# Router logits taken inside the output projection, shift added by matmuls in the turns, ranks by five wide products

## The chip, the cores and the metric

The program runs on one core of a Trainium2 chip. The metric is the device time of one execution in microseconds, the median of the runs shown. All data are float32. Engines are named as in the profile: PE is TensorE (PEld its weight loads), DVE VectorE, ACT ScalarE, POOL GpSimd, SP the engine that issues most DMAs.

## The reference, cut to what matters

The program is a chain of three model layers on a stream of 512 tokens by 1024 features. The change lies in the third, between the output projection of the mixer and the mixture of experts (MoE). In the kernel's symbols, with g, s and gate the adaptive scale, shift and gate of the layer:

```
h   = h + gate1 * (merged @ w_out)                    # the projection, 1024 x 1024
y   = h * rsqrt(mean(h*h) + eps) * norm2_g * (1 + g)  # norm and scale
y   = y + s                                           # shift
gl  = y @ w_group + b_group      # 4 group logits of a token
el  = y @ w_expert + b_expert    # 32 expert logits of a token
group = argmax(gl);  e1, e2 = top 2 of el inside that group
rank  = how many earlier token-choices took the same expert
out = h + gate2 * (w1 * expert_e1(y) + w2 * expert_e2(y)), then a final norm
```

An expert is `(silu(y @ w_gate) * (y @ w_up)) @ w_down` with 256 hidden features. Tokens are put into blocks of 64 by expert and rank, so the experts start only when every token has its expert and its rank.

## The kernel before, in words

The stream is kept transposed: tile `hT[:, k, :]` holds features 128k to 128k+127 on the partitions and the 512 tokens along the row; `xnT` is the same for the normed stream. Each engine runs one instruction list in program order, and they meet by semaphores. PSUM has eight banks; "tiles" 0, 1, 2, ... rotate over banks 0 to 3 (`open_tile` waits until the one four back is evacuated), 4 to 7 have fixed uses.

In `pe2`, after the 16 product pairs of the merge (`seven_pair`), PE waits until five of the seven products of the last pair are read and then runs the projection: eight tiles of eight matmuls of 128x512 (`dense_tile`, L1635). DVE adds each tile to `hT` (L1333) and ACT squares it. After the last tile this happens in a row:

- PE sums the squares over the partitions by matmuls with ones (`block_sums`, L1655); ACT takes the root (`root`), DVE the reciprocal (L2323), and PE spreads it over all partitions (`spread_inverse`, L1665).
- DVE multiplies the eight tiles by the inverse and by `GS2 = norm2_g * (1 + g)` into `xnT` (`apply_norm`, L2334), ACT adds the shift tile by tile (`shifts`).
- PE makes the 36 logits per token as one product of eight 36-column matmuls over 512 tokens (L803). ACT copies it, and PE turns it to token-major form in four pieces (L1677, `turn4`); DVE adds the bias (L1347) and starts the top-2 selection (L1352 to L1369).
- Behind that, PE turns `xnT` into token rows: 32 transposes of 128x128 in eight tiles, each evacuated by ACT into `XB`, and ACT sends them to the scratch `expert_in_scratch` (L958). Only then do the two exponentials of the router run on ACT.
- With the one-hots ready PE makes the ranks and counts: ten matmuls at L816 and four at L819, each 32 columns wide. DVE turns counts and ranks into slots (L1161 to L1407), with one compare and six compare-and-adds for the number of extra blocks; PE places the tokens in their blocks (L827), DVE writes the row index `X_ROW` (L1423), and POOL gathers the tokens of the first blocks by it (L622).
- PE in the meantime turns `hT` (32 transposes) and spreads the second gate (L832).

The experts follow in 24 slots (L842, L855, L865, L877), each with two experts' weights loaded by SP or gathered by POOL.

The order of the work is that of the lists written out in `pe2`, `act2` and `dve2`; there is no planner.

Of the kernel before, what the change touches and what calls it, by code (L numbers as in the profile page):

```python
# [22 lines left out]
P = 128  # L23
T = 512
# [60 lines left out]
def model_kernel(nc, t, out):  # L85

    ctx = ExitStack()
    with ctx:
# [249 lines left out]
        BR = work[:, 14 * T + 288:14 * T + 324]  # L338
        LGT = work[:, 15 * T:16 * T]
# [323 lines left out]
        def pe2(pe, ct, open_tile, take_chunk, dense_tile, norm_sum_in_rows, turn4, new_xn, attention, seven_pair):  # L663
# [130 lines left out]
            pe.wait_ge(sem("product_read"), 7 * (M_BASE[0] + 15) + 5)  # L794
            for n in range(KD):
# [5 lines left out]
            for k in range(KD):  # L801
                before(k)
                ins = pe.matmul(bank[0:36, :], WR[:, k, :], xnT[:, k, :], start=(k == 0), stop=(k == KD - 1))  # L803
            ins.then_inc(sem("logits"), 1)
            evacuated(pe, ct.tile - 1)
# [85 lines left out]
        def act2(act, ct, act_, take_tile, squares, square_tiles, root, attention, first_of_pair, shifts):  # L891
# [51 lines left out]
            squares(hT, arena(24, KD), first=lambda k: evacuated(act, t0 + k))  # L943
            ct.chunk, ct.tile = ct.chunk + KD, ct.tile + KD
            root()
            shifts(MOD[:, 24:32], KD)
            act.wait_ge(sem("logits"), 1)
            free_bank(act_(LGT[0:36, :], bank_of(ct.tile)[0:36, :], ACT.Copy), ct.tile)
            ct.tile += 1
            ct.tile += 1  # L950
            for a in range(TT):
                for half in range(2):
                    act.wait_ge(sem("h_turned"), 2 * a + half + 1)
                    free_bank(act_(XB[a][:, half * 512:(half + 1) * 512], bank_of(ct.tile)[:, :], ACT.Copy), ct.tile)
# [55 lines left out]
        EXTRA, ENDS, OFFSET, FIRST = [ebuf[:, 1, 128 + NE * j:160 + NE * j] for j in range(4)]  # L1010
        REACHED = ebuf[:, 0, 0:200].rearrange("p (c h) -> p c h", c=8)
# [141 lines left out]
        def dve2(dve, ct, link, take_tile, take_turned, apply_norm, add_to_h, copy_tiles, attention, quarter_sum, combine_pair):  # L1153
# [166 lines left out]
            for p in range(16):  # L1320
# [7 lines left out]
                if p % 4 == 3:  # L1328
                    for h in range(2):
                        V.tensor_tensor(MERGED[:, p // 4 * 2 + h, :], M_OUT[2][:, h, :], M_OUT[3][:, h, :], ADD).then_inc(sem("merged"), 1)  # L1330
            for k in range(KD):
# [6 lines left out]
            apply_norm(GS2, shifted=True)  # L1338
            V.tensor_tensor(G2DIAG.rearrange("p (k n) -> p k n", k=KD), ident[:, :].unsqueeze(1).broadcast_to([P, KD, P]),
                            MOD[:, 40:48].unsqueeze(2).broadcast_to([P, KD, P]), MUL).then_inc(sem("g2_diagonal"), 1)  # L1340
# [4 lines left out]
            ct.tile += 1  # L1345
            n = take_turned()
            free_bank(V.tensor_tensor(LG, bank_of(n)[:, 0:144].rearrange("p (q n) -> p q n", q=TT), BR.unsqueeze(1).broadcast_to([P, TT, 36]), ADD), n)  # L1347
            evacuated(dve, n)

# [31 lines left out]
            ts(FIRST, numbers, float(CAP), MUL)  # L1381
# [1511 lines left out]
```

## Time and profile before

| | us |
|---|---|
| median of 3 runs | 2554.71 |
| lowest, highest | 2551.04, 2558.86 |
| profiled execution, its own time | 2550.86 |
| its span | 2549.1 |
| PE busy | 2432.2 (95%) |
| DVE busy | 1389.8 (55%) |
| ACT busy | 488.9 (19%) |
| POOL busy | 788.0 (31%) |

The span runs from the first instruction to the last. A busy engine is not yet a bound: what sets the time is the chain of work that ended last. All starts below are in us from the start of the span. A float32 matmul has two records in the profile, a transpose on PE one.

### The profile page before, as it was taken

Reading aid. Unit: us, or ns where it says so; the run is one execution under the profiler, and the core shown is the slowest. Engines: PE = TensorE matmul, PEld = TensorE weight load, DVE = VectorE, ACT = ScalarE, POOL = GpSimd, SP = SyncE. Lnnn points to the kernel's source line nnn. Section 1 sums busy time; section 2 is a strip of 40 time slices with the busy share of each in tenths; the row PEclk is TensorE's granted clock in tenths of the full one; section 3 lists DMA queues with packets and bytes.
Section 4 is the critical chain, followed back from the end, with each engine's and each line's share of the span. In section 5 each row is a group of like instructions: output and inputs, shape, how many; then the busy total and the mean of one; then the engine's idle time right before and its main releaser. Section 6 shows DMA issues by size and latency. Waiting matters only on the chain.

```text
span 2549.1 us, 29161 instructions
## 1 busy us (share of the span) xinstructions
PE 2432.2 (95%) x10988; PEld 1589.8 (62%) x10988; DVE 1389.8 (55%) x2449; ACT 488.9 (19%) x1039; POOL 788.0 (31%) x704
## 2 busy tenths in 40 slices
PE   8998999999999999999999998999899999799995
PEld 6875468888864444588888843434557885433331
DVE  5558369877744663453467522798896432411113
ACT  2016121100022330211000112001584000311111
POOL 6410134454555017634454201000101540123331
PEclk9999999999999999899999999999899999799998
DMA  5320247732324223333332233533000336299993
GB/s 141 96 67 1 74 131 216 227 112 83 95 79 134 61 61 120 116 83 87 86 93 83 60 107 94 148 110 93 26 1 23 94 85 223 101 373 375 383 349 150
DMA packets 345970, 321.21 MB, mean 126 GB/s; under 512 B 32892, under 2 KB 319537, under 8 KB 333119
## 3 DMA queue, kind: packets, MB, share of 16 engines
q1 hardware_dynamic: 323340, 268.56, 33.2%
q10 hardware_dynamic: 5216, 27.27, 3.2%
q0 software_dynamic: 17280, 23.54, 2.8%
q8 instruction: 90, 1.47, 0.2%
q14 instruction: 44, 0.36, 0.0%
HBM read 354.52 MB, written 25.17 MB: 149 GB/s over the span
## 4 chain that ended last, share of the span: by engine, by line
PE 92%; DVE 4%; issue 1%; ACT 1%; DMA 1%; POOL 0%; SPq 0%; POOLq 0%; DVEq 0%; ACTq 0%
PE bank L1704 30%; PE bank L1635 25%; PE bank L1743 12%; PE bank L855 7%; PE bank L877 3%; PE bank L1814 2%; PE bank L1863 2%; PE bank L1845 2%; PE bank L842 1%; PE bank L1986 1%; PE bank L1655 1%; PE bank L686 1%; PE bank L723 1%; PE bank L733 1%; DVE work L2499 1%
## 5 line engine op out<-in xcount | busy, mean ns | idle before, releaser
L1635 PE MATMUL bank<-xnT,ring 128*128 128x512 f32 (+2 forms) x736 | 326.1, 601 | 7.6 <-ACT xnT L2055 4.5
L1704 PE MATMUL bank<-xnT,ring 128*128 128x256 f32 x1024 | 255.6, 387 | 8.3 <-ACT xnT L2055 5.9
L1635 PEld LDWEIGHTS bank<-xnT,ring 128*128 128x128 f32 (+2 forms) x736 | 137.2, 188 | 191.6 <-issue 187.2
L1704 PE MATMUL bank<-big,ring 128*128 128x256 f32 x1024 | 242.5, 380 | 0.0
L1704 PEld LDWEIGHTS bank<-xnT,ring 128*128 128x128 f32 x1024 | 196.3, 193 | 41.5 <-issue 10.9
L1704 PEld LDWEIGHTS bank<-big,ring 128*128 128x128 f32 x1024 | 193.9, 190 | 27.2 <-issue 1.2
L2055 ACT ACTIVATE rinv<-bank 128x256 f32<-128x256 f32 (+1 forms) x57 | 22.1, 388 | 792.6 <-PE bank L1704 621.5
L496 POOL TENSOR_TENSOR work<-ring 128x512 f32<-128x512 f32 x32 | 44.0, 1377 | 329.7 <-PE bank L1704 189.8
L2055 ACT ACTIVATE work<-bank 128x512 f32<-128x512 f32 (+2 forms) x195 | 104.7, 568 | 191.9 <-PE bank L1635 115.6
L2055 ACT ACTIVATE big<-bank 128x512 f32<-128x512 f32 (+1 forms) x78 | 41.8, 557 | 446.8 <-PE bank L1635 245.2
L1635 PE MATMUL bank<-big,ring 128*128 128x512 f32 x288 | 125.8, 599 | 0.1
L855 PE MATMUL bank<-big,work 128*64 128x512 f32 x384 | 116.8, 611 | 8.5 <-issue 7.3
L2387 DVE TENSOR_TENSOR xnT<-big 128x512 f32<-128x512 f32 x64 | 65.5, 1024 | 92.9 <-PE bank L1704 92.9
L2055 ACT ACTIVATE work<-work,nmax 128x512 f32<-128x512 f32 (+1 forms) x192 | 105.7, 556 | 35.5 <-DVE nmax L2499 35.4
L1635 PE MATMUL bank<-hT,ring 128*128 128x512 f32 x256 | 110.9, 593 | 0.0
L496 POOL TENSOR_TENSOR selw<-ring 128x512 f32<-128x512 f32 x32 | 42.6, 1331 | 198.9 <-PE bank L1704 190.1
L1434 DVE TENSOR_TENSOR work<-bank,causal 128x256 f32<-128x256 f32 x24 | 10.2, 425 | 165.9 <-ACT causal L2055 165.9
L1635 PEld LDWEIGHTS bank<-big,ring 128*128 128x128 f32 x288 | 55.3, 192 | 69.7 <-issue 68.9
L497 POOL TENSOR_TENSOR ring<-ring 128x512 f32<-128x512 f32 x64 | 94.7, 1480 | 0.0
L516 POOL TENSOR_TENSOR big<-ring 128x512 f32<-128x512 f32 (+1 forms) x16 | 18.1, 1133 | 239.7 <-PE bank L1743 211.2
L855 PEld LDWEIGHTS bank<-big,work 128*64 128x64 f32 x384 | 36.3, 141 | 83.9 <-issue 82.3
L877 PE MATMUL bank<-big,work 128*64 128x512 f32 x320 | 87.6, 598 | 0.6 <-ACT work L2055 0.6
(439 smaller groups left out, 4663.4 us busy)
## 6 DMA issues: line engine op xcount, KB each, us to landing
ring<-in_mlp_w_up_dram SPq DMA_DIRECT2D x64, 512.0 KB, 4.4
ring<-in_mlp_w_down_dram SPq DMA_DIRECT2D x64, 512.0 KB, 4.7
big<-in_moe_w_down_dram SPq DMA_DIRECT2D x32, 1024.0 KB, 9.5
work<-in_ada_w_dram ACTq DMA_DIRECT2D x32, 768.0 KB, 4.8
ring<-in_w_in_dram SPq DMA_DIRECT2D x40, 512.0 KB, 3.8
big<-in_moe_w_gate_dram SPq DMA_DIRECT2D x16, 1024.0 KB, 9.9
big<-in_moe_w_up_dram SPq DMA_DIRECT2D x16, 1024.0 KB, 11.9
ring<-in_moe_w_up_dram SPq DMA_DIRECT2D x16, 1024.0 KB, 14.9
```

Source lines behind the costliest of these rows:

```text
L496: G.tensor_tensor(s1, a21, a22, ALU.add).then_inc(sem("weights_added"), 1)
L497: G.tensor_tensor(a21, a11, a21, ALU.subtract).then_inc(sem("weights_turned"), 1)
L855: ins = pe.matmul(bank[h * CAP:(h + 1) * CAP, :].rearrange("p (g n) -> p g n", g=2), XTB[s % 2][:, k, h * CAP:(h + 1) * CAP], gu[h][:, k], ...
L877: ins = pe.matmul(banks[5 + c][h * CAP:(h + 1) * CAP, :], HTB[s % 2][:, k, h * CAP:(h + 1) * CAP], DN_OF[w][h][:, k * D + c * T:k * D + (c ...
L1635: ins = pe.matmul(bank[0:m, 0:n], w[:, q, :], rhs(k), start=(k == 0), stop=(k == total - 1))
L1704: ins = pe.matmul(product(r), left[r][:, kp, :], rhs(r, kp), start=(first and kp == kps[0]), stop=(last and kp == kps[-1]), skip_group_che ...
L1743: ins = pe.matmul(product(r), left[r][:, k, :], rhs, start=(k == 0), stop=(k == half - 1), skip_group_check=True)
L1814: done.append(pe.matmul(o, q, k[:, 0:width], start=True, stop=not masked, skip_group_check=True))
L1845: ins = pe.transpose(banks[n % 3][:, at:at + P], probs(s, h, qi)[:, kb * P:(kb + 1) * P], ident[:, :])
L1863: ins = pe.matmul(o[h * HD:h * HD + m, kb * P:T], v, probs_turned(s, h, kb), start=(kb == 0 and not prior), stop=(kb == TT - 1 and last_of ...
L2055: return nc.scalar.activation(out_, in_, func, **kw)
L2387: V.tensor_tensor(t1, b12, b11, ALU.subtract).then_inc(sem("quarters"), 1)
```

## The change

- The projection is preceded by a wait for all seven products of the last pair. Three times inside it, after tiles 2, 4 and 6, PE makes the logit matmuls of two finished feature tiles, and the last two after the sums of squares. They read `xnT = GS2 * hT`, which ACT now makes right behind each square; the norm's inverse is not in it. Even and odd tiles go to the rows 0 to 35 and 64 to 99 of bank 5.
- The logits of the shift alone, `s @ w`, are eight 36-wide matmuls into bank 6. `rstd` is turned to one number per token by a 4-wide matmul, and DVE takes the reciprocal as `RINVT`. The turn of the logits adds the two halves by a product with `HALVES`. DVE multiplies by `RINVT` and adds the bias, in two operations.
- `apply_norm`, the spreading of the inverse, and `shifts` are gone here. A root on a constant stands ahead of the squares on ACT.
- The shift as a row on all partitions, divided by the inverse later, comes from two 512-wide matmuls with ones against a diagonal (`SHIFTDIAG`), copied by ACT. In each of the eight turns of `xnT` a one-row matmul, `rstd` of the tokens by that row, 512 wide, opens the bank, and four ordinary matmuls against the identity add the turned blocks. ACT multiplies by `RINVT` as it evacuates.
- Ranks and counts are five matmuls: one of 160 columns, then 128, 96, 64 and 32.
- The number of extra blocks is one compare over 7 x 32 and one reduction. `G2DIAG` is made ahead of the projection.

```diff
-            norm_sum_in_rows(arena(24, KD))
-            before = new_xn()
-            pe.wait_ge(sem("router_loaded"), 64)
+                if n in (2, 4, 6):
+                    logits(n - 2)
+                    logits(n - 1)
+            sum_in_rows(arena(24, KD))
+            for k in range(KD):
+                pe.matmul(banks[6][:, 0:36], MOD[:, 24 + k:25 + k].broadcast_to([P, P]), WR[:, k, :], start=(k == 0), stop=(k == KD - 1))
+            logits(KD - 2)
+            logits(KD - 1).then_inc(sem("logits"), 1)
+            pe.wait_ge(sem("stat_read"), ct.n["norm"])
+            pe.matmul(banks[6][:, 64:68], rstd[:, 0:P], ident[:, 0:P:32], start=True, stop=True, skip_group_check=True).then_inc(sem("inverse_wide"), 1)
...
-            turn4(lambda a: LGT[0:36, a * P:(a + 1) * P], rows_=36)
-
+            for a in range(TT):
+                ins = pe.matmul(bank[:, 36 * a:36 * (a + 1)], LGT[0:100, a * P:(a + 1) * P], HALVES[0:100, :], start=True, stop=True)
+            ins.then_inc(turned, 1)
+            for c in range(2):
+                bank = open_tile()
+                pe.matmul(bank[:, :], ones[:, :], SHIFTDIAG[:, c * T:(c + 1) * T], start=True, stop=True).then_inc(sem("h_turned"), 1)
+            for c in range(2):
+                evacuated(pe, SHIFT_TILE + c)
             for a in range(TT):
                 for half in range(2):
-                    turn4(lambda k: xnT[:, 4 * half + k, a * P:(a + 1) * P], done="h_turned")
+                    bank = open_tile()
+                    pe.matmul(bank[:, :], rstd[32 * a:32 * a + 1, 0:P], SHIFTROW[32 * a:32 * a + 1, half * T:(half + 1) * T], start=True, stop=True, skip_group_check=True)
+                    for k in range(4):
+                        ins = pe.matmul(bank[:, k * P:(k + 1) * P], xnT[:, 4 * half + k, a * P:(a + 1) * P], ident[:, :], start=False, stop=True,
+                                        skip_group_check=True)
+                    ins.then_inc(sem("h_turned"), 1)
...
-            for a in range(TT):
-                for c in range(a + 1):
-                    ins = pe.matmul(bank[:, a * NE:(a + 1) * NE], ones[:, :] if c < a else BEFORE[:, :], RE[3][:, c, :],
-                                    start=(c == 0), stop=(c == a))
+            pe.matmul(bank[:, 0:P + NE], BEFORE[:, :], RE3_ZEROS, start=True, stop=False, skip_group_check=True)
             for c in range(TT):
-                ins = pe.matmul(bank[:, P:P + NE], ones[:, :], RE[3][:, c, :], start=(c == 0), stop=(c == TT - 1))
+                later = TT - c
+                to = bank[:, (c + 1) * NE:(TT + 1) * NE].rearrange("p (a n) -> p a n", a=later)
+                ins = pe.matmul(to, ones[:, :], RE[3][:, c, :].unsqueeze(1).broadcast_to([P, later, NE]), start=False, stop=(c == TT - 1),
+                                skip_group_check=True)
...
+            act_(SSQ[:, 0:1], EPSC, ACT.Sqrt)
+            for k in range(KD):
+                evacuated(act, t0 + k)
+                act_(arena(24, KD)[:, k, :], hT[:, k, :], ACT.Square).then_inc(sem("squares"), 1)
+                act_(xnT[:, k, :], hT[:, k, :], ACT.Identity, scale=GS2[:, k:k + 1]).then_inc(sem("xn"), 1)
...
-            ts(EXTRA, counts, float(CAP), ALU.is_gt)
-            for c in range(2, T // CAP):
-                stt(EXTRA, counts, float(CAP * c), EXTRA, ALU.is_gt, ADD)
+            tt(FULL, counts.unsqueeze(2).broadcast_to([P, NE, T // CAP - 1]), FULL_AT.unsqueeze(1).broadcast_to([P, NE, T // CAP - 1]), ALU.is_gt)
+            link(V.tensor_reduce(EXTRA, FULL, AX, ADD))
```

## Rows read from the trace of the kernel before

**Rows 1.** The page, part 4: the chain that ended last, by engine.
```profile
PE 92%; DVE 4%; issue 1%; ACT 1%; DMA 1%; POOL 0%; SPq 0%; POOLq 0%; DVEq 0%; ACTq 0%
```
**Rows 2.** Timeline of PE: start, duration, line, operation, out<-in, shape, count [idle before].
```profile
2118.09 55.17 PE L1635 MATMUL bank<-work,ring 128*128 128x512 f32 x128
2173.19 2.00 PE L1655 MATMUL bank<-big,ones 128*32 128x128 f32 x64
2177.53 1.16 PE L1665 MATMUL bank<-rinv,ident 128*128 128x128 f32 x8 [2.34 <-DVE rinv L2323]
2180.37 9.99 PE L803 MATMUL bank<-xnT,work 128*36 128x512 f32 x16 [1.68 <-ACT xnT L2055]
2191.05 0.44 PE L1677 MATMUL bank<-ident,work 36*128 36x36 f32 x4 [0.68 <-ACT work L2055]
2191.41 3.99 PE L1677 MATMUL bank<-ident,xnT 128*128 128x128 f32 x32
2198.16 0.41 PE L816 MATMUL bank<-work,before 128*128 128x32 f32 x2 [2.75 <-DVE work L1369]
...
2200.80 1.89 PE L819 MATMUL bank<-work,ones 128*128 128x32 f32 x8
...
2211.42 1.94 PE L827 MATMUL bank<-work 128*128 128x24 f32 x16 [0.74 <-DVE work L1407]
2213.20 3.33 PE L832 MATMUL bank<-work,ones 128*128 128x512 f32 x4
```
**Rows 3.** Timeline of DVE, the same columns.
```profile
2116.77 1.88 DVE L2411 TENSOR_TENSOR work<-bank,work 128x256 f32<-128x256 f32 x5
...
2173.30 0.75 DVE L1333 SCALAR_TENSOR_TENSOR hT<-bank,small,hT 128x512 f32<-128x512 f32 x1 [6.12 <-PE bank L1635]
...
2191.59 0.31 DVE L1347 TENSOR_TENSOR work<-bank,work 128x144 f32<-128x144 f32 x1 [5.12 <-PE bank L1677]
...
2199.70 0.17 DVE L1371 TENSOR_REDUCE small<-work 128x4 f32<-128x16 f32 x1 [1.60 <-ACT small L2055]
...
2202.80 0.19 DVE L1161 TENSOR_SCALAR work<-bank 128x32 f32<-128x32 f32 x1 [1.21 <-PE bank L819]
2203.03 1.32 DVE L1165 SCALAR_TENSOR_TENSOR work<-bank,work 128x32 f32<-128x32 f32 x6
...
2208.06 0.37 DVE L1157 TENSOR_TENSOR work<-work,rows 128x200 f32<-128x200 f32 x1
...
2214.60 0.18 DVE L1423 CAST small<-work 128x24 uint32<-128x24 f32 x1
```
**Rows 4.** Timeline of ACT, the same columns.
```profile
2174.73 1.28 ACT L2055 ACT_TABLE_LOAD   x1
...
2196.59 1.09 ACT L2055 ACTIVATE selw<-bank 128x512 f32<-128x512 f32 x2 [0.40 <-ACT work L2055]
...
2198.06 1.28 ACT L2055 ACT_TABLE_LOAD   x1 [0.39 <-ACT selw L2055]
```
**Rows 5.** Windows, router stretch: length, busy (records) by PE, PEld, DVE, ACT, POOL, clock, DMA.
```profile
2180.00:2184.00 4.00, 3.63 (x5) 0.93 (x6) 4.00 (x7) 4.00 (x7) 0.00 (x0) 0.50 0.00 0
...
2200.00:2203.00 3.00, 3.00 (x17) 3.00 (x17) 1.55 (x9) 0.00 (x0) 0.00 (x0) 0.50 0.00 0
...
2206.00:2211.00 5.00, 4.22 (x20) 3.99 (x20) 4.55 (x14) 2.97 (x7) 0.00 (x0) 0.58 0.01 3
```
**Rows 6.** Timeline of PE early in the program: matmuls of eight rows.
```profile
174.88 9.62 PE L1925 MATMUL bank<-work,selw 8*128 8x512 f32 x16
```
**Rows 7.** Windows of that stretch: length, PE busy (records), clock, DMA share, GB/s.
```profile
176.00:178.00 2.00, 2.00 (x6) 1.00 0.00 0
...
180.00:182.00 2.00, 2.00 (x4) 0.50 0.00 0
```
**Rows 8.** Timeline of PE in the expert slots.
```profile
2234.17 7.09 PE L855 MATMUL bank<-ring,work 128*64 128x512 f32 x32 [1.18 <-ACT work L2055]
...
2252.45 0.59 PE L855 MATMUL bank<-hT,work 128*64 128x512 f32 x1
2252.97 0.51 PE L865 MATMUL bank<-ident,work 128*128 128x128 f32 x2
```

More of the change, by code:

```diff
@@ L338, in model_kernel @@
         BR = work[:, 14 * T + 288:14 * T + 324]
+        BIAS = work[:, 14 * T + 324:14 * T + 360]
+        HALVES = work[:, 14 * T + 360:14 * T + 396]
+        SHIFTDIAG, SHIFTROW, RINVT = work[:, 8 * T:10 * T], work[:, 18 * T:20 * T], small[:, 596:600]
+        SHIFT_TILE = 194
         LGT = work[:, 15 * T:16 * T]
@@ L794, in pe2, with logits @@
             pe.wait_ge(sem("product_read"), 7 * (M_BASE[0] + 15) + 5)
+            before = new_xn()
+            def logits(k):
+                before(k)
+                at = 64 * (k % 2)
+                return pe.matmul(banks[5][at:at + 36, :], WR[:, k, :], xnT[:, k, :], start=(k < 2), stop=(k >= KD - 2), skip_group_check=True)
+            pe.wait_ge(sem("router_loaded"), 64)
+            pe.wait_ge(sem("product_read"), 7 * (M_BASE[0] + 16))
             for n in range(KD):
                 dense_tile([KD], lambda k: MERGED[:, k, :], before=(lambda k: pe.wait_ge(sem("merged"), k + 1)) if n == 0 else None)
-            norm_sum_in_rows(arena(24, KD))
@@ L798, in pe2 @@
-            before = new_xn()
-            pe.wait_ge(sem("router_loaded"), 64)
-            bank = open_tile()
[L801 to L805, printed above, removed]
-            turn4(lambda a: LGT[0:36, a * P:(a + 1) * P], rows_=36)
+                if n in (2, 4, 6):
+                    logits(n - 2)
+                    logits(n - 1)
@@ L942, in act2 @@
             t0 = ct.tile
-            squares(hT, arena(24, KD), first=lambda k: evacuated(act, t0 + k))
+            act_(SSQ[:, 0:1], EPSC, ACT.Sqrt)
[3 more added lines that the diff above has]
+                act_(xnT[:, k, :], hT[:, k, :], ACT.Identity, scale=GS2[:, k:k + 1]).then_inc(sem("xn"), 1)
             ct.chunk, ct.tile = ct.chunk + KD, ct.tile + KD
             root()
-            shifts(MOD[:, 24:32], KD)
             act.wait_ge(sem("logits"), 1)
-            free_bank(act_(LGT[0:36, :], bank_of(ct.tile)[0:36, :], ACT.Copy), ct.tile)
+            act_(LGT[0:100, :], banks[5][0:100, :], ACT.Copy).then_inc(sem("logits"), 1)
             ct.tile += 1
-            ct.tile += 1
+            act.wait_ge(sem("rinv"), ct.n["norm"])
+            for c in range(2):
+                act.wait_ge(sem("h_turned"), c + 1)
+                free_bank(act_(SHIFTROW[:, c * T:(c + 1) * T], bank_of(ct.tile)[:, :], ACT.Copy), ct.tile)
+                ct.tile += 1
             for a in range(TT):
                 for half in range(2):
-                    act.wait_ge(sem("h_turned"), 2 * a + half + 1)
-                    free_bank(act_(XB[a][:, half * 512:(half + 1) * 512], bank_of(ct.tile)[:, :], ACT.Copy), ct.tile)
+                    act.wait_ge(sem("h_turned"), 2 * a + half + 3)
+                    free_bank(act_(XB[a][:, half * 512:(half + 1) * 512], bank_of(ct.tile)[:, :], ACT.Copy, scale=RINVT[:, a:a + 1]), ct.tile)
                     ct.tile += 1
@@ L1337, in dve2 @@
             ct.step("squares", KD)
[L1338 to L1340 removed]
+            ct.step("norm")
             link(V.memset(RI[0][:, 0:1], 1000.0))
@@ L1344, in dve2 @@
                 ts(RI[0][:, 1 << lv:2 << lv], RI[0][:, 0:1 << lv], float(1 << lv), ADD)
-            ct.tile += 1
+            dve.wait_ge(sem("router_loaded"), 64)
+            dve.wait_ge(sem("inverse_wide"), ct.step("wide"))
+            V.reciprocal(RINVT, banks[6][:, 64:68]).then_inc(sem("rinv"), 1)
+            link(V.tensor_tensor(BIAS, banks[6][:, 0:36], BR, ADD))
+            dve.wait_ge(sem("rinv"), ct.n["norm"])
             n = take_turned()
-            free_bank(V.tensor_tensor(LG, bank_of(n)[:, 0:144].rearrange("p (q n) -> p q n", q=TT), BR.unsqueeze(1).broadcast_to([P, TT, 36]), ADD), n)
+            tt(LG, bank_of(n)[:, 0:144].rearrange("p (q n) -> p q n", q=TT), RINVT.unsqueeze(2).broadcast_to([P, TT, 36]), MUL)
+            free_bank(V.tensor_tensor(LG, LG, BIAS.unsqueeze(1).broadcast_to([P, TT, 36]), ADD), n)
             evacuated(dve, n)
+            ct.tile += 2
+            link(V.memset(RE3_ZEROS[:, P:P + NE], 0.0))
             def one_hot(logits, n, top, out_, scratch, c):
```

17 lines of the change are left out of this document (14 added, 3 removed).

## The prediction

> **What bounds the kernel now.** I read the chain that ended last first: PE carries 92% of it [rows 1], so a cut on another engine pays only where PE waits. I then looked for PE's waits around the edited lines in its timeline. The projection ends at 2118.09 + 55.17 = 2173.26 [rows 2]; call that moment E. From there to the last index, 2214.60 + 0.18 = 2214.78 or E + 41.5 [rows 3], the work is a relay between engines, and PE sits idle 2.34, 1.68, 0.68, 2.75 and 0.74 us in it [rows 2]. The experts' token gather hangs on that index, so the stage after it moves rigidly with it. The weights of the first slots lie there already. The question is thus where the index comes after the change.
>
> The relay before: the root waits for a table load of 1.28 [rows 4], the inverse is spread by E + 5.4 (2177.53 + 1.16), the logits take 9.99 from 2180.37 [rows 2], and the bias operation starts at 2191.59, E + 18.3 [rows 3]. The ranks end at 2200.80 + 1.89 = 2202.69 [rows 2], and the first step behind them starts at 2202.80, E + 29.5 [rows 3].
>
> **Up to the projection's end.** PE now also waits for the last products of the merge. The last read ends at 2116.77 + 1.88 = 2118.65 [rows 3], where PE started at 2118.09 [rows 2]: 0.6 later. A pair of logit matmuls goes to two column groups. In the experts 32 records of such pairs take 7.09 [rows 8], 0.43 for two records side by side, so a pair costs 0.86 (one behind the other: 1.72, the upper bound). The array changes from one shape of tile to another before and after. Price from a row: the last 64-column record starts at 2252.45, at 0.43 the next would be 2252.88, and the first 128-column one starts at 2252.97 [rows 8], so 0.09 a change. Three pairs: 3 x (0.86 + 0.18) = 3.1. The projection ends at E + 3.7; call that E'. What DVE does extra ahead of it (the diagonals, 1.2 each) lies in its idle 6.12 between tiles [rows 3]; I cost it at nothing, and without that cover it would be 2.5.
>
> **From there to the logits.** The last tile goes through DVE (0.75) and ACT's square and is ready at E' + 1.47, as before: the table load came then, at 2174.73 [rows 4]. That load is now ahead of the projection, but the stream's scaling sits before the root, 0.6. PE's sums end at E' + 1.9 (2175.19) [rows 2]. Eight shift matmuls of 36 columns: I take 0.12 a record, the pace of the spread (1.16 less a tail of 0.28, over 7 [rows 2]), 16 records, 1.9; to E' + 3.8. The last pair with its changes 1.05, to 4.9. The copy on ACT 0.6 with two handovers, to 5.6. The four-piece turn, 8 records, 1.0, to 6.6. The bias step can start at E' + 6.7 = E + 10.4 against E + 18.3. **The logits come 7.9 earlier.**
>
> **The turns.** Before, they were 32 records in 3.99 [rows 2] and PE then waited 2.75 for the one-hots. The selection takes 6.5 and stays. In the changed list PE first makes the shift row, two 512-wide matmuls, 1.72, to E' + 8.3, and waits for ACT to copy the second, 0.65: E' + 9.0. Then eight tiles. The one-row matmul is 512 wide; 16 records of eight-row ones of that width took 9.62 [rows 6], of which about half at the lower clock [rows 7], which fits 0.43 a record at the upper level and 0.86 at the lower, so few rows save nothing: 0.86. Four ordinary matmuls are eight records where transposes were four: 8 x 0.12 = 0.96. Two changes of tile shape, 0.18. A tile is 2.0, eight 16.0, and the turns end at E' + 25.1 = E + 28.8, where they ended at 2195.40, E + 22.1, before. Bounds: 0.5 a tile if it cost what transposes did (4.0 in all), 3.6 a tile at half clock (29 in all). I take 2.0 because its rows are of the same width.
>
> Now what was hidden is late. The one-hots are ready by E' + 13.6 and wait. On ACT the two exponentials stand behind the last of the eight evacuations: it ends 0.65 after the turns; in the trace the last one ended at 2196.59 + 1.09 = 2197.68 [rows 4] and DVE went on at 2199.70 [rows 3], 2.0 for a DMA issue, a table load of 1.28 [rows 4] and the two exponentials. DVE then had 1.9 of small steps and now has 2.2 (the table of limits and a memset). So the step behind the ranks starts 0.65 + 2.0 + 2.2 = 4.9 after the turns, at E + 33.7, **4.2 later than before.** The five wide products (records of at most 160 columns, 1.3 in place of 2202.69 - 2198.16 = 4.5 [rows 2]) are done 3.5 before that and give nothing.
>
> **Behind the ranks.** Seven compares took 0.19 + 1.32 with gaps, 2202.80 to 2204.35, and a memset 0.1 [rows 3]. Two operations of 224 elements replace them, about 0.4 each by the 0.37 of one with 200 [rows 3]: 0.9 saved. PE turns the residual right behind the ranks and is then idle for some 7 us until the block placement. After PE's idle stretches the clock stood at 0.50 (2200 to 2203 [rows 5]), the 1.2 GHz level, and 32-column records cost 0.21 there (8 in 1.89) against 0.12. The placement's 16 records took 1.94 and were waited for [rows 2]; at the lower level 3.6: +1.7 (0 if the clock stays up).
>
> **The sum.** +4.2 - 0.9 + 1.7 = +5.0, rounded down to +4.5 for the 0.12 pace, which has tails in it. The first expert product met the lower clock before and meets it again: no term. Against the profiled execution: span 2549.1 to 2553.6, own time 2550.86 to 2555.4. That execution lies 3.8 below the median of the runs, 2554.71. The forecast for the median is 2554.7 + 4.5 = 2559.2, call it 2559.
>
> On the clock one rule bears. Turns of 128 rows raised it here: from 2206 PE does nothing but transposes and the stretch to 2211 averages 0.58, so it came back inside it [rows 5]. The Trainium skill, "TensorE: Matmul & The Clock Gate", Part 4, says that transposes in the engine's transpose mode do not count as busy for the clock. By that rule ordinary matmuls in their place would hold the clock in the turns better than before; the trace does not agree, so I give it no gain; with either, the sum above stands, and only the first rival below would be less likely.
>
> **Rivals.**
> (a) The clock falls in the turns. For: matmuls of eight rows left PE busy 2.00 of 2.00 and yet the clock went from 1.00 to 0.50 among them [rows 7], and half of each new tile is a one-row matmul. The stretch ahead, with 36-column work and two waits, is thin too: in such work the clock was 0.50 before [rows 5]. Against: the other half has all rows. Price: 3.6 a tile for 2.0, eight times, 12.8; if it falls after a tile or two, 11. It decides from about the second tile on. Time 2570 to 2572: slower.
> (b) The logit pairs do not run side by side: 4 x 0.86 = 3.4 more, 2562.5. Against: the paired records [rows 8].
> (c) The tiles cost what the transposes did, 4.0, with the one-row matmul beside the others. The turns then end at E' + 13, ACT's copies, 0.55 each, soon after, and DVE goes on near E + 21.7: 7.8 earlier, less 0.9, plus 1.7, so -7.0, 2547.7. For: tiles on different rows can overlap. Against: the four matmuls use all 128 rows and write the same bank.
> (d) The change does not do what it says: a square or the scaling needs another table than the root's, and the load is back, 1.3 more: 2560.3. It joins the forecast's range.
>
> **How the numbers follow.** Chances: forecast with (d) 0.64, (a) 0.20, (b) 0.09, (c) 0.07. 0.3% is 7.7 us, about what a measurement of this kernel can tell from none: no change is 2547.0 to 2562.4. The runs of before spread by 4 to either side, so the forecast gives 0.53 to no change, 0.09 to slower and 0.02 to faster; (a) is slower; (b) splits 0.05 and 0.04; (c) 0.03 no change and 0.04 faster. Together faster 0.06, same 0.61, slower 0.33. The range goes from 2552, which leaves out most of (c), to 2573, which takes in (a); the forecast's own is 2554 to 2564.
>
> **What would show it.** Right: the bias step 6.5 to 8 us after the projection's end; eight turn tiles of 1.9 to 2.1; the exponentials directly behind the last evacuation, and the ranks' product ended while DVE still waits for ACT; the placement's records at 0.21. Wrong: turn tiles of 3.6 at clock 0.50 (a), or of about 0.5 (c); logit records that start 0.43 apart one by one (b); or an index less than E + 40 behind the old E.

## The result, and the profile after

| | before | after |
|---|---|---|
| median (lowest to highest), us | 2554.13 (2551.04 to 2558.86), 6 runs | 2573.85 (2569.97 to 2576.69), 6 runs |
| profiled execution, own time | 2550.86 | 2569.97 |
| its span | 2549.1 | 2568.2 |

The change makes the kernel slower: ratio 1.0074, 95% interval 1.0064 to 1.0085, or 19.7 us by the medians. The forecast was 2559; the measured time is 1.9 above what rival (a) gave (2570 to 2572), and 0.85 above the range's upper end of 2573.

I start where [rows 2] stood, with PE's timeline of the router stretch after (start, duration, line, operation, out<-in, shape, count, and in brackets the idle time before).

```profile
2121.13 20.84 PE L1683 MATMUL bank<-work,ring 128*128 128x512 f32 x48 [0.97 <-DVE work L2459]
2141.89 1.05 PE L804 MATMUL bank<-xnT,work 128*36 128x512 f32 x4
...
2179.78 2.00 PE L1703 MATMUL bank<-big,ones 128*32 128x128 f32 x64
...
2188.98 1.09 PE L834 MATMUL bank<-work,rstd 1*128 1x512 f32 x2 [0.73 <-issue]
2190.00 1.16 PE L836 MATMUL bank<-ident,xnT 128*128 128x128 f32 x8
2191.09 1.27 PE L834 MATMUL bank<-work,rstd 1*128 1x512 f32 x2
2192.29 2.07 PE L836 MATMUL bank<-ident,xnT 128*128 128x128 f32 x8
2194.30 2.07 PE L834 MATMUL bank<-work,rstd 1*128 1x512 f32 x2
2196.30 2.08 PE L836 MATMUL bank<-ident,xnT 128*128 128x128 f32 x8
...
2218.20 0.74 PE L842 MATMUL bank<-work,before 128*128 128x160 f32 x2
2218.73 1.22 PE L846 MATMUL bank<-work,ones 128*128 128x128 f32 x8
...
2231.18 2.02 PE L855 MATMUL bank<-work 128*128 128x24 f32 x16 [0.99 <-DVE work L1455]
```

A turn tile is the one-row product (the two records of L834) and the four ordinary products behind it (the eight records of L836). The first tile costs 2191.09 - 2188.98 = 2.1, as forecast; from the third on each costs 4.0, 2.00 for each of its two groups (2194.30, 2196.30 and so on). The eight run from 2188.98 to 2218.20, 29.2 us. The projection is L1683 now, its sums of squares L1703. E', the moment at which the projection ends and the sums start, is 2179.78.

The windows of that stretch, to be held against [rows 5] and [rows 7] (length; busy time and records of PE, PEld, DVE, ACT, POOL; granted clock; DMA share; GB/s):

```profile
2190.00:2195.00 5.00, 5.00 (x20) 3.54 (x20) 3.24 (x12) 1.28 (x2) 0.00 (x0) 0.69 0.00 0
2195.00:2200.00 5.00, 5.00 (x12) 2.28 (x10) 0.00 (x0) 0.78 (x2) 0.00 (x0) 0.50 0.26 105
...
2220.00:2225.00 5.00, 1.30 (x12) 1.06 (x10) 3.26 (x16) 2.77 (x7) 0.00 (x0) 1.00 0.25 103
```

PE is busy 5.00 of 5.00 and yet the granted clock is 0.50, the 1.2 GHz level, from 2195 to 2215. It is back at 1.00 only when the turns are over. This is the pattern of [rows 7], in a place where the index, the row numbers by which POOL gathers the tokens, hangs on it.

DVE's timeline after, whose rows answer to [rows 3]:

```profile
2186.59 0.31 DVE L1194 TENSOR_TENSOR work<-bank,small 128x144 f32<-128x144 f32 x1 [1.20 <-PE bank L823]
...
2193.30 0.28 DVE L1417 TENSOR_TENSOR work<-work 128x128 f32<-128x128 f32 x1
2221.16 0.17 DVE L1419 TENSOR_REDUCE small<-work 128x4 f32<-128x16 f32 x1 [27.57 <-ACT small L2103]
...
2223.45 0.39 DVE L1194 TENSOR_TENSOR work<-bank,work 128x224 f32<-128x224 f32 x1
...
2234.45 0.18 DVE L1471 CAST small<-work 128x24 uint32<-128x24 f32 x1
```

ACT's timeline after at the end of its copies, which answers to [rows 4]:

```profile
2218.45 0.69 ACT L2103 ACTIVATE selw<-bank,small 128x512 f32<-128x512 f32 x1 [3.32 <-PE bank L836]
...
2219.52 1.28 ACT L2103 ACT_TABLE_LOAD   x1 [0.39 <-ACT selw L2103]
```

DVE has the one-hots at 2193.30 + 0.28 = 2193.58 and then waits 27.57 us for ACT's exponentials. They stand behind the table load, that behind the last evacuation, and that behind the last turn tile. The index is ready at 2234.45 + 0.18 = 2234.63; before it was 2214.78 [rows 3]. That is 19.85 later, of which 2.15 lies ahead of the change's first instruction: the last products of the merge start at 2119.13, and at 2116.98 in the trace of before. This is a difference between two executions; in e6, which is the kernel before up to the ranks, the same products start at 2121.82. The other 17.7 lie between the start of the projection and the index. The profiled spans differ by 19.1, so behind the index nothing more is lost.

### The profile page after: what moved, and what is told of

Its sections match the earlier page's. It is cut to its first block, busy times and chain, and to the rows that moved or that the text cites. A ratio compares the mean times of both kernels' runs of the same rounds, so it can differ in the third digit from the quotient of the medians.

```text
span 2568.2 us, 29256 instructions
## 1 busy us (share of the span) xinstructions
PE 2452.3 (95%) x11036; PEld 1602.2 (62%) x11036; DVE 1389.2 (54%) x2442; ACT 490.8 (19%) x1042; POOL 787.3 (31%) x704
## 4 chain that ended last, share of the span: by engine, by line
PE 93%; DVE 4%; issue 1%; ACT 1%; DMA 1%; POOL 0%; SPq 0%; ACTq 0%; POOLq 0%; DVEq 0%
PE bank L1752 30%; PE bank L1683 25%; PE bank L1791 12%; PE bank L883 7%; PE bank L905 3%; PE bank L1862 2%; PE bank L1893 2%; PE bank L1911 2%; PE bank L870 1%; PE bank L1703 1%; PE bank L2034 1%; PE bank L690 1%; PE bank L727 1%; PE bank L836 1%; PE bank L834 1%
## 5 line engine op out<-in xcount | busy, mean ns | idle before, releaser
L1683 PE MATMUL bank<-xnT,ring 128*128 128x512 f32 (+2 forms) x736 | 327.7, 603 | 6.5 <-ACT xnT L2103 4.5
L1683 PEld LDWEIGHTS bank<-xnT,ring 128*128 128x128 f32 (+2 forms) x736 | 137.4, 189 | 191.9 <-issue 187.8
L2103 ACT ACTIVATE work<-bank 128x512 f32<-128x512 f32 (+1 forms) x191 | 102.7, 567 | 191.0 <-PE bank L1683 115.5
L1683 PE MATMUL bank<-big,ring 128*128 128x512 f32 x288 | 125.8, 599 | 0.1
L2103 ACT ACTIVATE work<-work,nmax 128x512 f32<-128x512 f32 (+1 forms) x192 | 105.7, 556 | 35.2 <-DVE nmax L2547 35.1
L1683 PE MATMUL bank<-hT,ring 128*128 128x512 f32 x256 | 110.9, 593 | 0.0
L1683 PEld LDWEIGHTS bank<-big,ring 128*128 128x128 f32 x288 | 55.3, 192 | 69.7 <-issue 68.9
```

Of the source, the lines that this page charges most:

```text
L1683: ins = pe.matmul(bank[0:m, 0:n], w[:, q, :], rhs(k), start=(k == 0), stop=(k == total - 1))
L2103: return nc.scalar.activation(out_, in_, func, **kw)
```

## The experiments

All times of an experiment stand beside runs of the kernel before on the same chip. In the first three the shift's row in the turns is the question: is it the width of the one-row product, its few rows, or its being there at all?

**e1: all rows.** The same sum, but the factor is a 128-row matrix with `rstd` in one row and zeros elsewhere, made by four small DVE operations.

```diff
-pe.matmul(bank, rstd[32 * a:32 * a + 1, 0:P], SHIFTROW[32 * a:32 * a + 1, ...], start=True, ...)
+pe.matmul(bank, MASKED[:, a * P:(a + 1) * P], SHIFTROW[:, ...], start=True, ...)
```

> The changed kernel with the one-row matmul of each turn tile taken over all 128 rows: its stationary operand is the same row of roots with zeros in the other 127 rows (four small operations on DVE make it). Same width, same number of records, same output. Theory 1 (the clock falls because few rows are active): the clock stays at 1.00 in the turns, a tile costs 0.86 + 0.96 = 1.8, eight 14.6 where they took 29.3, the time falls from 2573.9 to about 2559. Theory 2 (the tiles cost what they cost by their width and their weight loads, and the clock falls in any such mix): the clock falls all the same, a tile stays near 3.6 to 4.0, the time is 2571 or more.

Measured: 2559.18 (2555.29 to 2562.08, 10 runs), ratio 1.0015 (1.0004 to 1.0026). One tile and the start of the next in PE's timeline (timelines and windows have the columns given above in all that follows):

```profile
2194.54 1.02 PE L835 MATMUL bank<-work 128*128 128x512 f32 x2
2195.40 1.05 PE L837 MATMUL bank<-ident,xnT 128*128 128x128 f32 x8
2196.30 1.02 PE L835 MATMUL bank<-work 128*128 128x512 f32 x2
```

A window of the same kernel in the middle of the turns:

```profile
2200.00:2205.00 5.00, 5.00 (x30) 3.57 (x29) 0.00 (x0) 2.06 (x3) 0.00 (x0) 1.00 0.27 108
```

The clock stays at 1.00, a tile costs 1.76, and the time is 14.7 below that of the change (ratio to before 1.0015 against 1.0074) with the same output and as many matmul instructions of the same width. The profiled execution is the slowest of the ten, 2562.08, and its merge ended late (the last products start at 2122.88), so the gain is read from the medians and from the tile. The median is also the forecast's time, within 0.2. So neither the width of the product nor the order of the work brings the clock down. What differs is the rows, and with them the changes of tile shape, which e1 doesn't have; e9 and e10 part the two.

**e2: no row.** The one-row product is taken out and the first turned block opens the bank; the shift is missing from the experts' input, nothing else.

> The changed kernel without the one-row matmuls (the shift is left out of the experts' input; the routing is untouched). Theory 1: clock 1.00, a tile 1.0, eight 8; the turns end some 21 us earlier and the time is about 2553. Theory 2: the clock falls in the ordinary products alone, a tile 2.0, eight 16, about 2561.

Measured: 2549.92 (2548.55 to 2554.27, 10 runs), ratio 0.9992 (0.9982 to 1.0002). All 64 records of the turns are one group:

```profile
2189.97 7.38 PE L835 MATMUL bank<-ident,xnT 128*128 128x128 f32 x64 [0.73 <-issue]
```

That is 0.115 a record and 0.92 a tile, at a clock of 1.00. The product for the shift thus costs 0.84 a tile in e1 (1.76), 1.2 in the change's own form while the clock holds (2.1), and 3.1 in the change's tiles at the lower clock (4.0).

**e3: transposes.** As e2, and the four products are transposes again, as before the change.

> As the run before, and the ordinary products against the identity are transposes again (the shift is left out of the experts' input). What the turns cost in all: both theories put them at 4.0 on PE, held to about 5.5 by the evacuations on ACT of 0.69 each; the index then hangs on the selection and the exponentials, and the time is 2550 to 2552: the logits part of the change alone is worth 3 to 5 us against 2554.1. If this run stays above 2560, the loss is not in the turns.

Measured: 2552.55 (2547.84 to 2556.45, 10 runs), ratio 0.9996 (0.9987 to 1.0006). In its profiled execution the clock was down before the turns and up in them, by PE's timeline:

```profile
2187.62 3.54 PE L828 MATMUL bank<-work,ones 128*128 128x512 f32 x4
2191.89 2.81 PE L835 MATMUL bank<-ident,xnT 128*128 128x128 f32 x24 [0.73 <-issue]
```

The shift row's two products take 3.54 in place of 1.96. In windows of 1 us the clock is 0.60 in 2190 to 2191 and 1.00 from 2191 on, so it was back before the first transpose; the 24 transposes go at 0.117 a record, the upper level, and don't bring it down. Ordinary products need twice the records (7.38 against some 4.3 with PE's waits for ACT's copies), but that lies beside DVE's selection, and the time isn't higher. So the products in place of transposes are not what made the change slow. Whether transposes do less for the clock than ordinary products stays open: e3's executions have mean clocks of 0.969 to 0.974, e2's of 0.973 to 0.976. In the two traces the clock fell in PE's wait for DVE behind the ranks and came back at 2210 to 2211 in e2 and at 2218 in e3; there both kernels run the same instructions, so the difference of the means need not come from the turns.

**e4: rows together.** The turns go by halves; the four one-row products of a half, which lie on rows 0, 32, 64 and 96 and write four banks, are issued one behind the other ahead of the 16 products.

```diff
-for a in range(TT):
-    for half in range(2):
-        bank = open_tile()
-        pe.matmul(bank, <row of a>, ...)
-        <4 products>
+for half in range(2):
+    four = [open_tile() for a in range(TT)]
+    for a in range(TT):
+        pe.matmul(four[a], <row of a>, ...)
+    for a in range(TT):
+        <4 products into four[a]>
```

> The full function. The four one-row matmuls of one half lie on four different row groups and write four banks; here they are issued together and the products follow, so there are 2 groups of four and 4 changes of tile shape in place of 8 single ones and 16. Theory 1: the four run side by side, 0.86 a group, the clock stays up: 2 x 1.05 + 8 x 0.96 = 9.8 in place of 29.3, about 2555. If they run one after the other with the clock up: 15, about 2560. Theory 2 (clock falls in any mix): 19 or more, 2563 or more.

Measured: 2553.08 (2549.52 to 2557.71, 10 runs), ratio 0.9999 (0.9989 to 1.0009). PE's timeline of the turns:

```profile
2189.00 1.14 PE L834 MATMUL bank<-work,rstd 1*128 1x512 f32 x8 [0.78 <-ACT work L2105]
2190.07 3.84 PE L837 MATMUL bank<-ident,xnT 128*128 128x128 f32 x32
2194.78 1.14 PE L834 MATMUL bank<-work,rstd 1*128 1x512 f32 x8 [0.87 <-ACT selw L2105]
```

Eight records of one row each take 1.14 together: the four row groups work side by side, where one product alone took 1.09. The clock is 1.00 in both halves of this execution. PE spends 2 x 1.14 in one-row products, where eight one by one take 8 x 1.09 at this clock, and the loss of 19.7 is gone. That the change has no gain then is a question of its own, taken up in e11.

**e5: 32 rows.** The one-row product reads 32 rows of the same numbers (the row divided by 32), all else as in the change. **e10: 64 rows** is e1 with 64 of its 128 rows, and **e9: two sides** is e1 with the 128-row product written as two of 64 columns side by side.

```diff
-pe.matmul(bank, rstd[32 * a:32 * a + 1, 0:P], SHIFTROW[32 * a:32 * a + 1, ...], ...)
+pe.matmul(bank, rstd[32 * a:32 * a + 32, 0:P], SHIFTROW[32 * a:32 * a + 32, ...], ...)   # e5
+pe.matmul(bank, MASKED[r:r + 64, a * P:(a + 1) * P], SHIFTROW[r:r + 64, ...], ...)       # e10
+for side in (0, 64):                                                                     # e9
+    pe.matmul(bank[side:side + 64], MASKED[:, a * P + side:a * P + side + 64], SHIFTROW[:, ...], ...)
```

> The changed kernel with 32 rows in place of the one row of the first matmul of each turn tile (the same root stands in 32 rows; the shift row is divided by 32, the output is the same). Width, records, group of rows and the 16 changes of tile shape are those of the changed kernel; only the number of active rows differs. If the clock follows the number of rows, it stays up, and a tile costs 2.1 (0.86 + 0.96 + two changes of shape), 0.3 more than with all rows: about 2561. If the shape changes or the narrow row group bring the clock down, a tile is 4.0 as in the changed kernel: 2573.

> As e1, with 64 rows of the same data in the product that opens a turn tile (1 row: 2573.9, clock fell; 32 rows: 2567.4, clock fell in the profiled run; 128 rows: 2559.2, clock stayed). Theory A1 (the clock depends on how much of the array works, by degrees): 64 rows lie between 32 and 128 and nearer to 128, clock at 1.00 for most of the turns, 2558 to 2564. Rival A2 (anything below all rows counts as little): clock 0.50 in the turns as in the changed kernel, 2567 to 2574.

> As the one with all rows (e1), but the 128-row product that opens each turn tile is written as two of 64 columns side by side, so the array changes its tile shape twice a tile as in the changed kernel, and as many instructions are issued. Theory A (few rows let the clock fall): all 128 rows are in use, so the clock stays at 1.00 in the turns, a tile costs 1.75 to 1.95 and the time is that of e1, 2557 to 2562. Rival B (the changes of tile shape, not the rows, make the clock fall): the clock goes to 0.50, tiles of 3.5 to 4.0, 2568 to 2574.

Measured: e5 2567.36 (2561.86 to 2576.61, 6 runs), ratio 1.0053 (1.0035 to 1.0071); e10 2561.05 (2556.67 to 2565.52, 7 runs), 1.0028 (1.0016 to 1.0040); e9 2561.72 (2560.43 to 2566.54, 5 runs), 1.0037 (1.0023 to 1.0051). PE's timeline of e5, the first product of the second tile and of the third:

```profile
2190.43 1.25 PE L834 MATMUL bank<-work,rstd 32*128 32x512 f32 x2
...
2193.61 2.07 PE L834 MATMUL bank<-work,rstd 32*128 32x512 f32 x2
```

That of e10, the first product of the second tile, and a window of its turns:

```profile
2191.54 1.12 PE L836 MATMUL bank<-work 64*128 64x512 f32 x2
...
2195.00:2200.00 5.00, 5.00 (x28) 3.22 (x27) 0.00 (x0) 1.37 (x2) 0.00 (x0) 1.00 0.34 138
```

That of e9, one tile:

```profile
2191.09 1.08 PE L836 MATMUL bank<-work 128*64 128x512 f32 x4
2192.10 1.16 PE L838 MATMUL bank<-ident,xnT 128*128 128x128 f32 x8
```

With 64 rows, and with two column halves on all rows, the clock is 1.00 through the turns; so neither the changes of tile shape nor the number of instructions takes it down. With 32 rows the profiled execution (2573.45) lost it within the second tile. The six executions of e5 differ: their mean clocks run from 0.973 (2561.86) to 0.968 (2576.61), and by and large the time falls as the clock rises. That fits 32 rows holding the clock in some executions and not in others; no trace shows one of the fast ones. With one row the profiled executions of the change and of e7 lost it, and all six times of the change are 2569.97 or more. What these runs show is that products on 64 and 128 rows kept the clock and products within one group of 32 rows did not. They don't show that the number of rows counts inside such a group: one row and 32 rows use the same group, and the intervals of their ratios overlap (1.0064 to 1.0085, and 1.0035 to 1.0071).

e9 and e10 also price the change of tile shape. A tile costs 2.14 in e10 and 2.10 in e9, and 1.76 in e1: 0.36 for the two changes, 0.18 each, where the prediction had 0.09. Over eight tiles that is 2.9, and the medians lie 2.5 (e9) and 1.9 (e10) above e1's.

**e6: ranks alone.** The kernel before with only the five wide products and the one compare with its reduction.

> The kernel before with only the five wide products and the one compare with its reduction. The products take 1.4 in place of 4.5, but DVE then waits for the exponentials and its own small steps, so the step behind the ranks starts about 0.9 earlier, and the compare saves 0.9: 1.8 in all, 2552. The rival, that all 3.1 of the products count: 4.0 earlier, 2550. Both are within what the times can tell; the trace decides.

Measured: 2552.28 (2549.55 to 2556.46, 10 runs), ratio 0.9995 (0.9986 to 1.0005): too little to tell. In the trace the compare starts 10.41 behind the bias step (before 2202.80 - 2191.59 = 11.21 [rows 3]), and the index's last cast 10.90 behind the compare (before 11.80): from 2194.93 to the row below, and from there to 2216.24. So 0.8 comes from the ranks and 0.9 from the compare, the second as priced. DVE's timeline at the compare:

```profile
2205.34 0.39 DVE L1159 TENSOR_TENSOR work<-bank,work 128x224 f32<-128x224 f32 x1
```

No idle time stands ahead of it: the ranks are ready before DVE is.

**e7: late wait.** The change, with the wait for all seven merge products moved behind the third tile of the projection. One run, no interval.

> The changed kernel with the wait for all seven products moved from the start of the projection to the first logit matmuls. The idle time of 0.97 before the projection falls to 0.1 and nothing else moves: one look, judged on the trace.

Measured: 2575.68. The projection starts with no idle time, the 0.97 ahead of it is gone, and the time isn't lower; the turns are as in the change. Its PE timeline, from the turn of the logits' last stage on:

```profile
2185.71 3.66 PE L829 MATMUL bank<-work,ones 128*128 128x512 f32 x4
2190.10 1.09 PE L835 MATMUL bank<-work,rstd 1*128 1x512 f32 x2 [0.73 <-issue]
2191.12 1.16 PE L837 MATMUL bank<-ident,xnT 128*128 128x128 f32 x8
2192.21 1.74 PE L835 MATMUL bank<-work,rstd 1*128 1x512 f32 x2
2193.88 2.08 PE L837 MATMUL bank<-ident,xnT 128*128 128x128 f32 x8
```

The shift row runs at the lower level (3.66), the first tile at the upper one (1.02 and 1.09 a half), then it falls again and stays down. So the clock need not be low at the start of the turns to be lost in them: here it was 1.00 from 2190 to 2192. What makes it fall first, the one-row products or the stretch of small products and waits ahead of them, this run doesn't part; e11 bears on it.

**e8: POOL adds the shift.** Transposes as before, ACT's copy with the inverse, then POOL adds the shift row to each 128x1024 block and stores it (the row added is not the right one, since the first block overwrites the diagonal from which PE makes it; the instructions are the same, and the routing doesn't use it).

```diff
+link(G.tensor_tensor(XB[a], XB[a], SHIFTROW, ALU.add))
+pool.dma_start(x_dram[a * P:(a + 1) * P, :], XB[a])
```

> The full function. The turns are transposes of the scaled stream, ACT evacuates them with the inverse, the shift row comes behind the turns, POOL (idle there) adds it to the token rows in SBUF and stores them, and the wait of the projection is moved as in the run before. By theory 1 the turns are off the path; the index hangs on the selection and the exponentials and comes about 31 us after the projection's end, some 6 us earlier than in the kernel before: about 2548. If POOL's four additions (1.4 per 512 columns: some 11 us) and their stores end after the index, or slow DVE down, the gain is gone: 2554 or more.

Measured: 2554.29 (2550.94 to 2559.02, 11 runs), ratio 1.0000 (0.9990 to 1.0009). The profiled execution is the slowest of the eleven. In it PE and ACT are off the path, the exponentials are done at 2196.7, and then DVE is slow. POOL's timeline:

```profile
2198.54 2.35 POOL L654 TENSOR_TENSOR work<-work 128x1024 f32<-128x1024 f32 x1
2201.79 2.35 POOL L654 TENSOR_TENSOR work<-work 128x1024 f32<-128x1024 f32 x1
2205.03 2.35 POOL L654 TENSOR_TENSOR selw<-selw,work 128x1024 f32<-128x1024 f32 x1
```

DVE's timeline of the same kernel:

```profile
2198.32 2.62 DVE L1199 TENSOR_SCALAR small<-rows 128x24 f32<-128x24 f32 x1
...
2201.25 2.94 DVE L1198 TENSOR_SCALAR work<-work 128x32 f32<-128x32 f32 x2
...
2205.43 2.04 DVE L1437 TENSOR_TENSOR_SCAN work<-work 128x32 f32<-128x32 f32 x1
```

The three DVE rows took 0.18, 0.40 and 0.22 in e4. Each now ends just behind an add of POOL (2200.94 behind 2200.89; 2204.19 behind 2204.14; 2207.47 behind 2207.38): DVE doesn't go slower, it waits until POOL's instruction is over. The Trainium skill, "SBUF — State Buffer", section "SBUF: two separate sides", has a rule for it: DVE and POOL share a pair of ports as an exclusive lock, which one of them holds for the whole instruction while the other is blocked. The trace agrees in the three ends, 0.05, 0.05 and 0.09 behind those of the adds. Not every operation of DVE waits: a reduction that started at 2205.01 took its 0.39, with the add of 2205.03 beside it. With one more row of 0.75 for 0.17, 7.4 us are lost in this execution.

**e11: the way round.** Full function: e4 with the late wait, and an order in which nothing stands ahead of the index that it doesn't need. The ranks' product goes behind the first half of the turns, the second gate's rows and the placement ahead of the turns of the stream, all in fixed banks; DVE uses the exponentials only behind the index.

```diff
 <first half of the turns>
+<ranks, into bank 4>
 <second half of the turns>
-<ranks, into a rotating bank>
+<G2DIAG spread, into banks 6 and 7>
+<placement, into bank 5>
 <turns of hT>
-<placement>
-<G2DIAG spread>
...
-dve.wait_ge(sem("router_exp"), 2); <w1, w2>
 <slots, X_ROW, G2ROW>
+dve.wait_ge(sem("router_exp"), 2); <w1, w2>
```

> Full function. The four one-row products of a half side by side (as in e4, 2553.1), the wait for the merge's last products behind the third tile of the projection, the ranks' product right behind the first half of the turns in a bank of its own, the placement and the second gate's spread ahead of the turns of the stream in banks of their own, and DVE's use of the two exponentials behind the index. Theory (the path runs over the one-hots, the ranks and DVE, and what stood in it was PE's and ACT's order): DVE goes on with the ranks at 2195 to 2196 in place of 2203.05 + 2.2, the index comes 9 to 10 earlier than in e4, the first turn of gathered tokens at 2211 to 2213 in place of 2221.8, and the time is 2543 to 2546 (ratio 0.996). Rival B (the turns of the stream, now later, with ACT's eight copies, become what the experts wait for): half of it is left, 2548 to 2550. Rival C (the clock falls in PE's waits around the placement, or the first weights are late): 2550 or more, no gain on e4.

Measured: 2546.76 (2542.44 to 2549.18, 10 runs), ratio 0.9976 (0.9966 to 0.9985). It is faster than before by 6.5 us by the medians, and its median is 27 below the change's, on another chip. PE's timeline, and a window of its first half of the turns:

```profile
2186.44 3.44 PE L829 MATMUL bank<-work,ones 128*128 128x512 f32 x4
2190.67 1.14 PE L835 MATMUL bank<-work,rstd 1*128 1x512 f32 x8 [0.78 <-ACT work L2102]
2191.74 5.47 PE L838 MATMUL bank<-ident,xnT 128*128 128x128 f32 x32
2197.04 0.44 PE L846 MATMUL bank<-work,before 128*128 128x160 f32 x2
...
2206.03 1.97 PE L858 MATMUL bank<-work 128*128 128x24 f32 x16 [1.18 <-DVE work L1449]
...
2214.79 1.13 PE L872 MATMUL bank<-ident,work 128*128 128x128 f32 x8 [3.23 <-DMA work<-expert_in_scratch,small]
...
2190.00:2195.00 5.00, 4.33 (x28) 3.61 (x29) 4.34 (x19) 1.64 (x3) 0.00 (x0) 0.79 0.00 0
```

DVE's, where it goes on with the ranks:

```profile
2198.40 0.39 DVE L1195 TENSOR_TENSOR work<-bank,work 128x224 f32<-128x224 f32 x1 [3.46 <-PE bank L850]
```

Here too the clock fell, and twice: ahead of the turns (3.44 for 1.96) and in the first half (5.47 for 3.84). The second fall came at 2192.9, among the 128-row products and with the four one-row products over for a microsecond; some 3.3 us later, with nothing but 128-row products in between, the clock was back. e12 has the same, at 2190.4. So a fall near the start of the turns need not be the one-row products' doing: the stretch of small products ahead may bring it too, though the same stretch stands ahead of the turns in e1, e2, e4, e9 and e10, whose traces show no fall. The difference is in what follows: the change and e7, with a one-row product in each tile, didn't get the clock back while the turns went on, 27 us in the change. In e11 the two falls delayed the ranks by 3 only. DVE goes on with the ranks 3.5 after its last small step. The first turn of gathered tokens comes 35.1 behind E' (2179.73 here), in e4 42.1: 7.0 gained, 6.3 in the medians. I had expected 9 to 10 for the index; the 3 that the clock took are the rest.

**e12: placement last.** e11 with the turns of the stream back ahead of the gate's spread and the placement.

> As e11 (2546.8), but the eight turns of the stream stand ahead of the second gate's spread and of the placement on PE, as in the changed kernel. Theory (in e11 half of the gain is that the placement doesn't queue behind turns whose banks ACT can empty only after the exponentials): ACT begins those eight copies behind the table load, the eighth turn can open its bank only after four copies, so the placement comes 4 to 6 later than in e11 and with it the index and the first turn of gathered tokens: 2551 to 2553. Rival (the whole gain of e11 is the ranks' early product and DVE's order; the turns of the stream fit in while DVE works out the slots): 2547 to 2548, no difference that can be told from e11.

Measured: 2550.90 (2542.58 to 2553.20, 12 runs), ratio 0.9982 (0.9974 to 0.9991). Here E' is 2177.40. PE's timeline:

```profile
2204.65 2.40 PE L1724 MATMUL bank<-ident,hT 128*128 128x128 f32 x16 [1.82 <-ACT xnT L2102]
...
2208.60 1.86 PE L861 MATMUL bank<-work 128*128 128x24 f32 x16
```

PE waits 1.82 for ACT's copies, which stand behind the exponentials, and the placement starts 31.2 behind E' against 26.3 in e11. The first turn of gathered tokens comes 39.7 behind E' (2217.14), against 35.1 in e11 and 42.1 in e4. By the traces, then, 4.6 of the 7.0 that e11 gained on e4 are that order; the rest is the early ranks, DVE's order and the late wait together, which were not parted. The times agree only in their medians, which differ by 4.1: they are from different chips, and the intervals of the ratios overlap (e11 0.9966 to 0.9985, e12 0.9974 to 0.9991).

## Why the prediction was wrong, step by step

- **What bounds the kernel** held: the loss of the profiled execution (19.1) is the shift of the index (19.85) to within 0.75, as a stage that moves rigidly with the index would have it.
- **Up to the projection's end.** Predicted +3.7, measured +4.4. The start went from 2118.09 to 2121.13; less the 2.15 that is chance this is 0.9 (I had 0.6). The projection took 58.65 in place of 55.10, so the three pairs cost 3.55 (3.1). The records do run side by side (0.99 a pair with tails), so rival (b) is out; the changes of shape were too cheap at 0.09.
- **From there to the logits.** Predicted E' + 6.7, measured 2186.59 - 2179.78 = 6.8. No table load came back; (d) is out.
- **The turns: the step that failed.** "I take 2.0 because its rows are of the same width." The width was right, 2.1 for the first tile. But the tile was priced from a stretch in which half the records ran at the lower level [rows 6, 7], and I took the upper one for all eight. Measured 29.2 in place of 16.0: the term was 13.2 too low. e1, e9 and e10 show that neither the width, nor the number of instructions, nor the changes of tile shape make the difference, but the rows that the product spans. Of it 12.2 is the clock (29.2 against 17.0 in e10, which has as many changes of shape), 1.0 these changes. Rival (a) had the mechanism and, with 3.6 a tile and 2570 to 2572, nearly the price; it had the row of before that showed it, PE busy 2.00 of 2.00 at 0.50 [rows 7], and I gave it 0.20. The argument against it, that the other half of the tile has all rows, was no more than an argument: that half didn't bring the clock back. Its other reason, the thin stretch ahead, may have its part: in e11 and e12 the clock fell behind that stretch among products of all rows, but came back within the half. Which of the two makes it fall first was not parted. Rival (c) is out: even at the upper level a tile took 2.1, not 0.5.
- **Behind the turns.** Predicted 4.9 from the turns' end to the step behind the ranks, measured 2223.45 - 2218.20 = 5.25. The ranks' products ended 2219.95, 3.5 before, and gave nothing, as said.
- **Behind the ranks.** The compare saved 0.9 (e6). The +1.7 for the placement didn't come in this execution: its records took 2.02. It did come elsewhere (3.58 in e9), so it is a matter of chance, not of the change.
- **The remark on transposes.** The rise inside a run of transposes [rows 5] stands as read. Giving the new products no gain was right for the time: e2 and e3 don't differ by more than their intervals (0.9982 to 1.0002, and 0.9987 to 1.0006).
- **The sum.** Against the +5.0 of the prediction's sum: +0.7 for the projection, +13.2 for the turns, +0.35 behind them, -1.6 behind the ranks, together +17.7, which is 19.85 less 2.15. With the clock held the time comes near the forecast: e1 2559.18, e10 2561.05, which are 5.3 and 7.8 above before on their chips against the 4.5 of the forecast. That e1 meets it to 0.2 is in part luck: its form has no changes of tile shape, and the +0.7, the +0.35 and the -1.6, of which 1.7 is the placement that wasn't late, nearly cancel.

What the change was to gain is real and went elsewhere. The bias step comes at E + 4.4 + 6.8 = E + 11.2, where it was E + 18.3: 7.1 earlier (predicted 7.9). But the shift, added in the turns, put 12 us of PE work ahead of the exponentials even by the forecast's price (16.0 for 3.99), and 25 as it came; and the exponentials were the next wait. e11 gets the gain back, on top of e4's rows together, by taking the exponentials, the ranks and the placement out of that queue, not by making any of them faster.

## What to carry to other kernels

A matmul on one row cost here what its width costs (1.09 for 512 columns, 1.02 on all rows), and where such products filled half of a stretch, everything beside them ran at the lower clock too. Look in the kernel's own trace for a stretch in which PE is fully busy at half the clock, and see what it ran. Then try narrow products on different row groups side by side, or rows filled with zeros: the second cost four DVE operations here and bought 14.7 us. And when a relay is shortened at one place, list what each engine has queued ahead of the next handover before pricing the gain.

## What the runs showed of the hardware that was not expected

- Few rows and the clock: with 1 row 0.50 for over 20 us at PE 5.00 of 5.00 busy; with 32 rows times of 2561.86 to 2576.61 from one execution to the next; with 64 rows, and 128, 1.00 through the turns.
- With 128-row products alone a fall among the turns was over after some 3.3 us (e11, from 2192.9); with a one-row product in each tile it lasted until the turns ended (27 us).
- A change of tile shape costs 0.18 at the upper level (2.10 and 2.14 against 1.76 a tile), twice what the prediction read from [rows 8].
- Four one-row products of 512 columns on four row groups take 1.14 together, one alone 1.09.
- A POOL add of 128x1024, 2.35 long, held up small DVE operations until its end: 0.18 became 2.62. A reduction beside it (2205.01) kept its 0.39.
